# Two transformer blocks on one core: a dozen instructions moved in the first attention, the middle of the MLP, the strips and the rotations

## What is computed

```python
# first block
h = _rmsnorm(x, ln_mix_g[l]); proj = h @ w_in[l]
y_attn = _dsa_attention(q, k, v, iq, ik, iw, rel_bias)     # 8 heads, top-256 keys, blocks of 128 rows
y_hgrn = _rmsnorm(o, hgrn_norm_g) * silu(hg)               # 4 heads of 128
y_conv = cb * _short_conv(cc * ch, conv_w)
g = sigmoid(gates)
mixed = g[0] * (y_attn @ w_up_attn) + g[1] * (y_hgrn @ w_up_hgrn) + g[2] * (y_conv @ w_up_conv)
x = x + mixed @ w_out
x = x + square(relu(_rmsnorm(x, ln_mlp_g) @ w_mlp_up)) @ w_mlp_down
# second block
x_q, x_kv, k_rope_raw, gate_a, u_pool, gate_b = split(x @ w_in_2)
y_a = mla_branch(...) * silu(gate_a)     # rms_norm of x_q and x_kv, products, rotation of q and k, 4 heads
y_b = pool_branch(u_pool, ...) * silu(gate_b)
x = layer_norm(alpha * x + concat(y_a, y_b) @ w_out_2)
```

## Time and profile before

| what | value |
|---|---|
| median of 3 runs | 2299.01 us (2297.06 to 2300.14) |
| the profiled execution | 2299.54 us, of which the span is 2297.7 us |
| PE busy | 2235.4 us (97%) |
| DVE busy | 1694.5 us (74%) |
| POOL busy | 1195.4 us (52%) |
| ACT busy | 837.3 us (36%) |

### The profile page before, as it was taken

How to read it: one execution, slowest core, us unless ns; L and a number is a source line. 1 busy time by engine, 2 the same in 40 slices (tenths; PEclk the granted TensorE clock), 3 DMA queues, 4 the chain that set the end, 5 groups by cost and what they waited for, 6 DMA issues and landing times. The chain is left out here.

```text
span 2297.7 us, 29211 instructions
## 1 busy us (share of the span) xinstructions
PE 2235.4 (97%) x10722; PEld 1849.6 (80%) x10722; DVE 1694.5 (74%) x2037; ACT 837.3 (36%) x1165; POOL 1195.4 (52%) x895
## 2 busy tenths in 40 slices
PE   7999999999999999999999999899999999999998
PEld 5678888888888899787878888788888777778886
DVE  7899999986778354446587766677777866578777
ACT  4312243123334256213343333444343434344423
POOL 4136553333323266334478988998886678400140
PEclk9999999999999999999999999999999999999999
DMA  4121123633332422444234445654442212441231
GB/s 155 37 83 64 64 92 106 169 138 113 108 128 92 129 66 65 156 146 165 83 135 153 151 171 189 256 193 156 147 156 101 70 37 92 131 152 49 65 110 73
DMA packets 93733, 272.50 MB, mean 119 GB/s; under 512 B 8800, under 2 KB 25320, under 8 KB 87080
## 3 DMA queue, kind: packets, MB, share of 16 engines
q1 hardware_dynamic: 76544, 206.86, 26.8%
q10 hardware_dynamic: 17064, 63.99, 7.9%
HBM read 186.13 MB, written 83.90 MB: 118 GB/s over the span
## 5 line engine op out<-in xcount | busy, mean ns | idle before, releaser
L1247 PE MATMUL pair<-actA,w_hi 128*128 128x512 f32 x2016 | 624.5, 391 | 2.1 <-issue 2.1
L1247 PEld LDWEIGHTS pair<-actA,w_hi 128*128 128x128 f32 x2016 | 377.5, 188 | 81.4 <-ACT sq L1938 2.9
L1247 PE MATMUL pair<-actA,w_lo 128*128 128x512 f32 x1008 | 393.1, 390 | 0.0
L1066 POOL TENSOR_TENSOR pad<-pad 128x1 f32<-128x1 f32 x93 | 24.7, 266 | 585.3 <-PE pair L1247 506.4
L1585 PE MATMUL pair<-tring,wsp 128*128 128x512 f32 x1344 | 307.4, 391 | 8.1 <-issue 7.1
L1585 PEld LDWEIGHTS pair<-tring,wsp 128*128 128x128 f32 x1344 | 253.2, 189 | 62.2 <-issue 9.0
L1196 POOL TENSOR_TENSOR wsp<-wraw,wsp 128x512 fp32r<-128x512 f32 x124 | 188.8, 1523 | 75.5 <-ACT wsp L2205 75.1
L1247 PEld LDWEIGHTS pair<-actA,w_lo 128*128 128x128 f32 x1008 | 189.5, 188 | 39.8
L1070 POOL TENSOR_TENSOR w_lo<-raw,w_hi 128x1024 fp32r<-128x1024 f32 (+1 forms) x93 | 209.1, 2248 | 7.5
L1585 PE MATMUL pair<-tsp,wsp 128*128 128x512 f32 x768 | 184.2, 391 | 4.4 <-DVE tsp L2910 2.1
L2951 DVE TENSOR_TENSOR xB<-pair,xB 128x1024 f32<-128x1024 f32 x112 | 136.3, 1219 | 70.3 <-PE pair L1585 70.1
(11 more groups left out here) (454 smaller groups left out, 4530.2 us busy)
## 6 DMA issues: line engine op xcount, KB each, us to landing
wraw<-w_pair SPq DMA_DIRECT2D x41, 1024.0 KB, 6.0
raw<-w_in SPq DMA_DIRECT2D x62, 512.0 KB, 3.5
staged<-hid_d SPq DMA_DIRECT2D x56, 512.0 KB, 3.3
proj<-stage ACTq DMA_DIRECT2D x40, 512.0 KB, 2.6
hid_d<-hsum SPq DMA_DIRECT2D x16, 1024.0 KB, 5.0
gates<-proj ACTq DMA_DIRECT2D x18, 512.0 KB, 5.2
raw<-w_out SPq DMA_DIRECT2D x16, 512.0 KB, 3.5
hid_d<-hid SPq DMA_DIRECT2D x16, 512.0 KB, 2.8
```

The costliest lines, as they stand in the source:

```text
L1066: nc.gpsimd.tensor_tensor(pad[:, 0:1], pad[:, 1:2], pad[:, 1:2], ALU.add)
L1247: last = nc.tensor.matmul(pair[par][:, cols], w[:, slot, wk], x[:, cols], start=(k == 0 and i == 0), stop=(k == kt - 1 and i == 2))
```

## The change

- *Start of the first attention*: the first logits go ahead of the last HGRN2 statistic on PE, the first mask ahead of `finish` on DVE, the first softmax ahead of `store_y` on ACT; the PSUM tiles of logits, transposes and outputs are renumbered.
- *End of the first attention*: up unit 0 is issued in pieces between the last items (half 1 in pairs of matmuls, half 0 around the last `turn_out`). The weights of units 0 and 1 are loaded and split earlier, the gates are loaded once the last logits and values are done, ACT's sigmoid of the first gates goes ahead of the casts of `yT`, and DVE gates unit 0 between them.
- *Middle of the MLP*: step 17 runs P1 P5 P2 P6 P7 P3 P4; the high parts of operands 6 and 7 are cast earlier on ACT, that of operand 8 after P2; `load_pair(18)` goes ahead of the staged loads, which wait for `xB`.
- *Strips*: DVE's T1 differences move behind the last additions, the order of the low parts changes, and the T3 difference (four subtractions of 128x512) moves to POOL (`third_sum`).
- *Roots*: ACT's root of xkv moves from behind (step 39, P4) to behind (step 40, P6); on DVE the xkv norm goes behind the splits of xq.
- *Rotations*: the load of `cs` no longer waits for xkv's low parts; `low2` and `rope` alternate in another order.

```diff
-RUN += [(st, p) for st in range(1, STEPS) for p in ("P1", "P5", "P6", "P2", "P7", "P3", "P4")]
+RUN += [(st, p) for st in range(1, N_PAIR + 1) for p in ("P1", "P5", "P6", "P2", "P7", "P3", "P4")]
+RUN += [(N_PAIR + 1, p) for p in ("P1", "P5", "P2", "P6", "P7", "P3", "P4")]
+RUN += [(st, p) for st in range(N_PAIR + 2, STEPS) for p in ("P1", "P5", "P6", "P2", "P7", "P3", "P4")]
...
-        turn.append(max(r, turn[-1] + (2 if j >= 7 else 1)) if turn else r + 2)
+        if j == 8:
+            r = max(r, NO[N_PAIR + 1, "P2"])
+        turn.append(max(r, turn[-1] + (2 if j >= 7 and j != 9 else 1)) if turn else r + 2)
...
+            load_q(6)
+            load_units("w_up", FIRST["up"], 2, 4)
+            load_q(7)
+            sp.wait_ge(l1_ok, N_ATT)
+            load_gates(sp, 0)
+            sp.wait_ge(pv1_ok, N_ATT)
+            load_gates(sp, 1)
...
+                    load_pair(N_PAIR + 2)
+                    sp.wait_ge(x_in, 16 * (NT + 6))
...
+                if i in (48, 52):
+                    split_units(FIRST["up"] + (i - 48) // 4, 1, 4)
...
+            def third_sum():
+
+                pool.wait_ge(tsum_ok, T_SUMS + 4)
+                pool.wait_ge(lo_ok, 4 * NT + 4)
+                for k in range(4):
+                    nc.gpsimd.tensor_tensor(xB[:, k, HALF:S], xB[:, 4 + k, HALF:S], xB[:, k, HALF:S],
+                                            ALU.subtract).then_inc(summed, 1)
+                sums[0] += 4
...
+                if i == START[STEPS + 1]:
+                    third_sum()
...
+            logits1(0)
+            stat(("hg", HG_HEADS - 1), "mean128", 1)
+            product(N_IN - 1, (N_IN - 1) % 2, (N_IN - 1) // 2, 8, hA, lA, (1,), (4, 5, 6, 7))
...
+                if i >= N_ATT - 4:
+                    m = 2 * (i - N_ATT + 5)
+                    first_up(1, (m, m + 1))
...
+            first_up(0, range(6))
             turn_out1(NB - 1)
+            first_up(0, range(6, 12))
...
+                if at_run == NO[N_PAIR, "P2"]:
+                    split_hi(6)
+                    split_hi(7)
...
-                if i == NO[STEPS + 7, "P4"]:
+                if i == NO[STEPS + 8, "P6"]:
                     root(("stat", "xkv"), (squares_used, STAT_BASE["xq"] + 2), EPSV, rstd_kv[:, :])
-                if i == NO[STEPS + 8, "P6"]:
...
-                    act.wait_ge(lo_ok, base + 6)
...
+            mask1(0)
+            finish(HG_HEADS - 1)
...
             for k in range(4):
                 low(NT + k, ysp[:, 8 + k, 1, :], yT[:, k, :], ysp[:, 8 + k, 0, :])
+                if k == 1:
+                    gated_unit(0, 0, 0)
...
-                if st == STEPS - 1 and p == "P7":
-                    t_sum("T1", (0, 1))
-            t_sum("T1", (2, 3))
+            t_sum("T1", (0, 1))
             for c in range(4, 8):
                 final_lo(c)
+            t_sum("T1", (2, 3))
+            t_sum("T2")
             t_los("T1")
-            t_sum("T2")
             t_sum("T4")
             t_los("T2")
-            t_sum("T3")
             t_los("T3")
             t_los("T4")
...
-                if h < 2:
-                    rope(h)
-                for k in ((), (), (0,), (1, 2))[h]:
-                    rope_lo(k)
+                if h == 0:
+                    rope_lo(0)
+                elif h == 1:
+                    rope(0)
+                elif h == 2:
+                    rope(1)
+                    rope_lo(1)
```

More of the change, by code:

```diff
@@ L977, in _ @@
                 st = RUN[at_run][0]
-                if at_run == START[st] + 3 and st + 2 < ALL_STEPS:
+                if at_run == START[st] + 3 and N_PAIR < st < ALL_STEPS - 2:
                     load_pair(st + 2)
@@ L1402, in _ @@
                         split_mean(("hg", key[2]), "mean128")
-                    else:
-                        stat(("hg", key[2]), "mean128", 1)
                 elif key[0] == "iT":
@@ L1505, in turn_out1, with first_up @@
                 mm.then_inc(yT_ps, 1)
+            yh = lambda br: lambda k: ysp[:, 4 * br + k, 0, :]
+            yl = lambda br: lambda k: ysp[:, 4 * br + k, 1, :]
+            def first_up(half, parts):
+                n = FIRST["up"]
+                if half == 1 and parts[0] == 0:
+                    pe.wait_ge(w_split, n + 1)
+                    pe.wait_ge(branch_lo, 8)
+                cols = slice(half * HALF, (half + 1) * HALF)
+                for m in parts:
+                    k, i = divmod(m, 3)
+                    w, x = ((w_hi, yh(0)), (w_hi, yl(0)), (w_lo, yh(0)))[i]
+                    mm = nc.tensor.matmul(pair[n % 2][:, cols], w[:, n % 2, k * P:(k + 1) * P], x(k)[:, cols],
+                                          start=(m == 0), stop=(m == 11))
+                if half == 0 and parts[-1] == 11:
+                    mm.then_inc(unit_mm, 1)
             pe.wait_ge(k_in, 64)
             wait_done(pe, ("o", HG_HEADS - 1))
+            logits1(0)
+            stat(("hg", HG_HEADS - 1), "mean128", 1)
+            product(N_IN - 1, (N_IN - 1) % 2, (N_IN - 1) // 2, 8, hA, lA, (1,), (4, 5, 6, 7))
             wait_done(pe, ("stat", "hg", HG_HEADS - 1))
-            issued = 0
+            issued = 1
             for i in range(N_ATT + 1):
@@ L2165, in _ @@
             softmax1(0)
+            store_y(HG_HEADS - 1)
             spill_gate(N_IN - 1)
@@ L2173, in _ @@
                     act.wait_ge(pv1_ok, i - 1)
-                nc.scalar.copy(PT[i % 2][:, 0:w], pair[0][:, 0:w]).then_inc(t0_ok, 1)
-            act.wait_ge(yT_ok, NB)
-            act.wait_ge(branch_lo, 16)
-            his(0, [ysp[:, 8 + k, 0, :] for k in range(4)], [yT[:, k, :] for k in range(4)], None)
+                nc.scalar.copy(PT[i % 2][:, 0:w], pair[1][:, 0:w]).then_inc(t0_ok, 1)
             nc.scalar.preload_act_table_set("sigmoid_and_others")
@@ L2181, in _ @@
                 nc.scalar.activation(gates[:, j % 2, :, :], gates[:, j % 2, :, :], ACT.Sigmoid).then_inc(gate_ok, 1)
+                if j == 0:
+                    act.wait_ge(yT_ok, NB)
+                    act.wait_ge(branch_lo, 16)
+                    his(0, [ysp[:, 8 + k, 0, :] for k in range(4)], [yT[:, k, :] for k in range(4)], None)
                 if j + 2 < NT:
@@ L2324, in _ @@
                 for j in range(N_SPLIT):
-                    if T_TURN[j] == at_run:
+                    if T_TURN[j] == at_run and j not in (6, 7):
                         split_hi(j)
@@ L2772, in _ @@
             gate_o(HG_HEADS - 1)
-            finish(HG_HEADS - 1)
             def mask1(i):
@@ L2832, in _, with gated_unit @@
             dve.wait_ge(yT_ok, NB)
+            def gated_unit(i, jj, br):
+                n = FIRST["up"] + 3 * jj + br
+                par, hn = n % 2, i * 3 + n // 2
+                mx = mixed[:, i * 2 + jj, :] if isinstance(i, int) else \
+                    mixed[:, bass.ds(i * 2 + jj, 1), :].rearrange("p a n -> p (a n)")
+                dve.wait_ge(unit_mm, i * 6 + (n + 1))
+                if br == 0:
+                    dve.wait_ge(gate_ok, i * 2 + (jj + 1))
+                dst = mx if br == 0 else prod[:, br - 1, :]
+                V.tensor_tensor(dst, pair[par][:, :], gates[:, jj, br, :], ALU.mult) \
+                 .then_inc(unit_out[par], 1)
+                dve.wait_ge(unit_out[par], hn + 1)
+                if br == 1:
+                    V.tensor_tensor(mx, mx, prod[:, 0, :], ALU.add).then_inc(mix_step, 1)
+                if br == 2:
+                    dve.wait_ge(mix_step, i * 2 + (jj + 1))
+                    V.tensor_tensor(mx, mx, prod[:, 1, :], ALU.add).then_inc(mixed_ok, 1)
@@ L2833, in _ @@
             for k in range(4):
                 low(NT + k, ysp[:, 8 + k, 1, :], yT[:, k, :], ysp[:, 8 + k, 0, :])
-            first = FIRST["up"]
-            with dve.Fori(0, 3) as i:
+                if k == 1:
+                    gated_unit(0, 0, 0)
+            for jj in range(2):
+                for br in range(0 if jj else 1, 3):
+                    gated_unit(0, jj, br)
+            with dve.Fori(1, 3) as i:
                 for jj in range(2):
-                    mx = mixed[:, bass.ds(i * 2 + jj, 1), :].rearrange("p a n -> p (a n)")
@@ L2840, in _ @@
                     for br in range(3):
-                        n = first + 3 * jj + br
-                        par, hn = n % 2, i * 3 + n // 2
-                        dve.wait_ge(unit_mm, i * 6 + (n + 1))
-                        if br == 0:
-                            dve.wait_ge(gate_ok, i * 2 + (jj + 1))
-                        dst = mx if br == 0 else prod[:, br - 1, :]
-                        V.tensor_tensor(dst, pair[par][:, :], gates[:, jj, br, :], ALU.mult) \
-                         .then_inc(unit_out[par], 1)
@@ L3220, in _ @@
             norm2([(g, xq[:, g, :]) for g in range(1, 4)], "q_norm_2", rstd_q)
-            dve.wait_ge(rstd_ok, 13)
-            norm2([(g, xkv[:, g, :]) for g in range(2)], "kv_norm_2", rstd_kv)
             add_strip(STEPS + 8, "P2")
@@ L3228, in _ @@
```

(2 more changed lines are left out.)

57 lines of the change are left out of this document (25 added, 32 removed).

## The result

The changed kernel takes 2311.70 us, median of 5 runs (2310.03 to 2314.31); the kernel before, run beside it, 2300.14. The ratio is 1.0046 [1.0032, 1.0059]: slower by 0.46%, where 2290.7 was forecast. The profiled execution took 2314.31 (span 2312.5), 14.77 more than the one of before.

The account below looks back on a forecast made before the run. PE, busy 97% of the span, was taken as the bound, its stops and slow restarts the places to gain. The terms summed to -8.3 against 2299.54, so 2291.2, or 2290.7 from the median; 8-in-10 range 2279 to 2298.

Parts of the forecast that it names:

- C: Step 17, middle of the MLP: PE's stop moves behind two products, to product 123, with a slow restart; a loss of 1.3 us.
- C2: The rest of the MLP behind step 17; the prediction had no term for it, so 0.
- B: End of the first attention: up unit 0 fills PE's idle time and the half-clock stretch goes; a gain of 3.3 us.
- F: Rotations: of 4.4 us of waits for `low2`, 0.5 to 1.5 stay; forecast -2.6 us, E and F together 6.3 gained.
- D: First strips: a 1.30 us stop goes, but DVE's four T2 differences slow beside POOL's T3 difference; a loss of 0.9 us.
- A: Start of the first attention: the wait for ACT's root goes and ACT's parking comes earlier; a gain of 0.9 us.
- its low part of 1.84: Step in C: operand 8's low part on DVE, ahead of addition 122, takes 1.84 us.
- The rival by which the stop goes: Step 17: the stop really goes, C -8.4 instead of +1.3, total 2281.0 us; chance 0.17.
- The slower rival: First strips: twenty DVE operations, not four, take turns with POOL; D +12.1 instead of +0.9, total 2301.9 us; chance 0.06.
- next late is DVE: Step in B: PE's unit 2 waits for DVE's gating to free unit 0's tile; takes back 1.1 to 1.5 us.
- E: Last strips: with xkv's root moved, PE's 2.09 us stop and its 1.56 slow restart go; a gain of 3.7 us.
- the cap of the second attention: Its first logits start 18.23 us after q's last low part, expected 6.4 earlier, limiting E and F to 6.3 us.

## Why the prediction was wrong

In the profile C missed its forecast by 6.1, C2 by 5.0, B by 4.1, F by 4.0, D by 2.6 and A by 1.2. The middle is the loss against the kernel before, and half of the miss.

**C failed, in size.** The order of instructions that it foresaw is there: the stop ahead of product 123, the addition of 122 behind operand 8's low part. What failed is the term "its low part of 1.84": it measured 6.73. That is 4.9 of the 6.1 by which C missed. Most of the rest is the restart: from the start of product 123 to the end of the stage PE takes 10.90 at a granted clock of 0.74, where it took 8.25 at 1.00 before, 2.65 more and not 1.5. Where the low part was quick, C came out near the +1.3 forecast: +1.1 with POOL waiting, +1.4 in the one execution that had 1.84; with the raw weights late it was quick too, but POOL's pause of 2.65 came on top. The prediction had the contention in its own rows, priced it in D, and left it out in C. The rival by which the stop goes (0.17) fell for the reason it gives itself, the order of DVE and ACT; it took operands 8 and 9 split ahead to remove that.

**C2 was missed.** No term stood for the later operands. Moving operand 8 by the diff's `j != 9` shifts every turn behind it by one product: +5.0, and 0.0 with the parity restored. The table of turns, worked out for both kernels, shows it: operand 10 stands at 124 and not at 123, and so on.

**D was low.** The slower rival named the mechanism, DVE taking turns with POOL for twenty operations instead of four; the profile shows fifteen. Its price, +12.1, was too high: the new stops are 2.21 and 0.66 with a slow restart of 3.3, not 10.5 and 1.6. Measured +3.5 against +0.9. The kernel is slower, as that rival had it, but mostly by C.

**B failed at one wait.** No clock of 0.50 between 925 and 930, and unit 0 done early, as said. The step "next late is DVE" failed: next late were the weights of units 2 and 3, whose loads stand behind SP's new waits. I had followed the gates on that queue and not what is queued behind them. With the weights first and unit 0 gated first, B is -3.7.

**A** had the parking right (0.84 earlier; 0.9 forecast). In 5 of 15 profiles with this part the clock then fell to 0.50 and took the gain back (A +0.3 to +0.7), the changed kernel's among them; in the others A is -1.0 to -1.2. In those five PE stood 1.87 to 2.32 behind the parking, in the other ten 1.58 to 1.82.

**E was right**: -3.9 against -3.7, in all 15 profiles.

**F failed at the stall.** "0.5 to 1.5 to stay" was one stop of 4.64. I counted two halves of a rotation ahead of a `low2`; it was a whole one, and its low part at 3.26 instead of the 1.23 it takes where POOL stands idle. So the cap of the second attention was never reached.

The Trainium skill, "SBUF — State Buffer", section "SBUF: two separate sides", has VectorE and GpSimd share a port pair as a lock held for one instruction. The 1.72 of the strips come near to that: each side waits for the other in turn, which would make 1.9 of 0.62 and 1.28, an estimate. The 6.73 goes beyond it: one POOL instruction of 1.30 ahead of a low part of 1.2 would make 2.5, an estimate too.

## What to carry to other kernels

Where two helper engines share a resource, price what PE waits for by the other's whole unbroken row and not by one operation of it: a low part of 1.2 us was held for 5 to 12 more, and PE with it. Make the other engine wait for it explicitly. When loads or casts are moved past new waits, follow everything that is queued behind them, and print the order for the whole stretch that a table of turns governs, not only for the place meant.

## What the runs showed of the hardware

- A DVE subtraction with two SBUF operands, 1.21 to 1.23 us alone, took 6.73 to 6.75 in seven profiles, 9.95 in one and 12.99 in one, always until POOL's unbroken row of 1.3 us operations ended. With a wait on POOL it took 1.23. The same program did 1.84 in one execution and 6.74 in another; what decides who gets in stays open.
- At the start of the first attention, with the same instructions, a stop of PE of 1.90 was followed by a granted clock of 0.50 from 787 to 789 in the changed kernel's profile, and one of 1.81 by 1.00 in the second profile of the kernel with T3 on DVE. The length alone doesn't decide it everywhere: in the first strips 12 matmuls took 3.00 at a granted clock of 1.00 behind a stop of 2.04, and 4.41 at 0.64 behind one of 2.00 with the strips as before.
